# Second mixer's q, k and v as seven products of half matrices, with the residual parked in DRAM and all heads written out

## What is computed

```python
xn = rmsnorm(h, norm_mix[i])
proj = xn @ w_in                    # layer 1: 1024 -> 3 * 1024: q, k, v
q = proj[..., :1024].reshape(B, L, 8, 2, 64)
k = proj[..., 1024:2048].reshape(B, L, 8, 2, 64)
v = proj[..., 2048:].reshape(B, L, 8, 128)
q = partial_rope(_rms_f32(q, g_q), cos, sin) * 64 ** -0.5
k = partial_rope(_rms_f32(k, g_k), cos, sin)
p = softmax(q @ k.T)                # two maps per head
o = (p[0] - lam * p[1]) @ v
h = h + (_rms_f32(o, g_sub) * (1 - lambda_init)) @ w_out
h = h + (silu(xn2 @ w_gate) * (xn2 @ w_up)) @ w_down
```

## Time and profile before

| | before |
|---|---|
| median of the runs | 1862.98 us |
| profiled execution, span | 1860.4 us |
| TensorE busy | 1849.7 us (99%) |
| VectorE busy | 1235.1 us (66%) |
| ScalarE busy | 879.7 us (47%) |
| GpSimd busy | 1162.6 us (62%) |
| layer 0's FFN ends, mixer of layer 1 begins | at 905.6 us |
| mixer of layer 1, attention part | about 938 to 1326 us |

### The profile page before, as it was taken

One profiled execution on the slowest core, in us unless ns is written; L12 is line 12 of the kernel. 1 busy time (PEld: TensorE's weight loads), 2 busy tenths in 40 slices (PEclk: granted clock), 3 DMA queues, 4 the chain that ended last, 5 costly groups with the idle time before them and its releaser, 6 DMA issues.

```text
span 1860.4 us, 31456 instructions
## 1 busy us (share of the span) xinstructions
PE 1849.7 (99%) x10845; PEld 1742.0 (94%) x10845; DVE 1235.1 (66%) x2072; ACT 879.7 (47%) x1855; POOL 1162.6 (62%) x1533
## 2 busy tenths in 40 slices
PE   9999999999999999999999999999999999999999
PEld 8888889999999999999988888888889999999998
DVE  6756566768576757576876666666587575756663
ACT  6444343455444445454444444444465454444553
POOL 4453644468687878788843333333558788887885
PEclk9999999999999999999999999999999999999999
DMA  8789997549697977774475666664233535353534
GB/s 270 257 240 237 222 259 173 183 108 228 209 237 238 235 227 218 250 232 118 107 145 121 126 124 124 130 118 91 74 90 110 148 99 157 100 153 101 154 112 133
DMA packets 380153, 309.51 MB, mean 166 GB/s; under 512 B 14395, under 2 KB 322398, under 8 KB 379766
## 3 DMA queue, kind: packets, MB, share of 16 engines
q1 hardware_dynamic: 349472, 237.81, 42.1%
q0 software_dynamic: 28416, 69.21, 20.5%
q10 hardware_dynamic: 2134, 0.82, 0.2%
HBM read 302.16 MB, written 144.04 MB: 240 GB/s over the span
## 4 chain that ended last, share of the span: by engine, by line
PE 91%; DVE 5%; ACT 1%; issue 1%; DMA 1%; POOL 0%; SPq 0%; ACTq 0%; DVEq 0%; POOLq 0%
PE ps L974 51%; PE ps L884 26%; PE ps L1155 3%; PE ps L1312 3%; PE ps L1280 2%; PE ps L1302 1%; PE ps L1130 1%; PE ps L1214 1%; DVE rstd L1502 1%; PE ps L1164 1%; DVE sx L1554 0%; PE ps L1244 0%; DVE mx L2077 0%; DVE gt L1661 0%; DMA wk<-in_x_prompt_dram 0%
## 5 line engine op out<-in xcount | busy, mean ns | idle before, releaser
L974 PE MATMUL ps<-sx,wh 128*128 128x400 f32 (+1 forms) x2044 | 530.3, 340 | 0.9 <-POOL wl L808 0.5
L808 POOL TENSOR_TENSOR wl<-raw,wh 128x256 fp32r<-128x256 f32 (+1 forms) x432 | 355.6, 855 | 97.9 <-ACT wh L2243 96.4
L774 POOL CAST wh<-raw 128x256 fp32r<-128x256 f32 x248 | 102.5, 456 | 450.6 <-PE ps L884 424.9
L974 PEld LDWEIGHTS ps<-sx,wh 128*128 128x128 f32 x2044 | 373.4, 188 | 3.0 <-ACT gt_first L2258 0.9
L974 PE MATMUL ps<-sx,wl 128*128 128x400 f32 (+1 forms) x1022 | 347.6, 340 | 0.0
L808 POOL TENSOR_TENSOR wl<-raws,wh 128x256 fp32r<-128x256 f32 x328 | 283.8, 910 | 84.4 <-ACT wh L2243 84.0
L1715 DVE TENSOR_TENSOR h<-h,ps 128x400 f32<-128x400 f32 (+1 forms) x280 | 154.5, 559 | 131.5 <-PE ps L974 131.4
L974 PE MATMUL ps<-fx,wh 128*128 128x400 f32 (+1 forms) x904 | 235.3, 341 | 0.1
L884 PE MATMUL ps<-xh,wh 128*128 128x512 f32 (+1 forms) x752 | 211.2, 357 | 0.0
L884 PE MATMUL ps<-xl,wh 128*128 128x512 f32 (+1 forms) x752 | 207.3, 349 | 0.0
L778 POOL TENSOR_TENSOR wl<-raw,wh 128x256 fp32r<-128x256 f32 x248 | 198.8, 831 | 5.1
(11 more groups left out here) (330 smaller groups left out, 3552.0 us busy)
## 6 DMA issues: line engine op xcount, KB each, us to landing
in_sums<-in_ffn_w_in_dram SPq DMA_DIRECT2D x16, 1536.0 KB, 10.7
raw<-in_sums SPq DMA_DIRECT2D x96, 256.0 KB, 3.0
in_sums<-in_ffn_w_in_dram SPq DMA_DIRECT2D x16, 1280.0 KB, 7.2
raw<-in_ffn_w_in_dram SPq DMA_DIRECT2D x80, 256.0 KB, 3.0
raws<-in_sums SPq DMA_DIRECT2D x80, 256.0 KB, 3.1
raw<-out_sums SPq DMA_DIRECT2D x120, 128.0 KB, 2.6
raws<-in_ffn_w_in_dram SPq DMA_DIRECT2D x52, 256.0 KB, 3.1
raw<-in_m_w_in_dram SPq DMA_DIRECT2D x24, 512.0 KB, 4.8
```

The lines of the kernel that those rows point to most:

```text
L774: ins = pool.tensor_copy(wh[:, slot, c], raw[:, slot, c])
L808: ins = pool.tensor_tensor(slot_of(n, 1)[:, c], raw_of(n)[:, c], slot_of(n, 0)[:, c].bitcast(F32), ALU.subtract)
L974: mm = pe.matmul(product_bank(layer, s, j), slot_of(n, low_w)[:, k * P:(k + 1) * P], x, start=(j in OPENS and k + q == 0), stop=(k == tile ...
```

## The change

- **q, k, v.** The 24 blocks become 84 products (`mix_product`) of 12 matmuls of 128x400: seven for each of eight key-value jobs (k and v of one head are the two output halves) and seven for each of four query jobs (two heads). The first 14, key-value and query alternating, stand before attention; the rest in the 13 places of the heads by `HALVES`, a place counting half products of 6 matmuls.
- **Tokens.** `mix_part` takes the place of `high_and_square` and `low_and_squares`: for a tile of the lower four ScalarE makes a scaled copy and two highs, VectorE one sum and two lows; for its partner ScalarE a scaled copy and five highs, VectorE three sums and five lows. `axe`, `axo`, `an` are single buffers, so a pair waits for the pair before.
- **Weights.** Sums are made in DRAM during the FFN: 8 copies on SyncE, 8 accumulating DMAs on GpSimd. Eight of the copies for layer 1's FFN move into the mixer. Loads are 256 KB; there are four slots. For the first 14 products ScalarE makes the high parts (`mix_high`), afterwards GpSimd makes both.
- **Read-out.** Four of the seven products are copied out of PSUM by ScalarE (`mix_copy`), the others added by VectorE (`mix_add`). The root of the mean square is no longer applied to q and k. Instead epsilon is scaled by token: 14 small matmuls against `rstd` (`token_norms`), and one matmul more per head ahead of the square sums (`eps_sums`). v gets its root in `values`: eight activations in place of three.
- **Residual.** `h` is stored to DRAM tile by tile as its square is made (`keep_last`, eight stores of 400 KB); its tiles then hold q, `at` and the outputs of heads 0 to 5. ScalarE's `mix_high(4)` waits for all eight stores. In the last head six outputs are split again (`split_y`, six on ScalarE, six on VectorE), and the tiles of `h` are loaded back and awaited in `add_tile`.
- **Order.** All eight heads are written out. The three k tiles behind the first scores of head 0 are gone.

The core of the diff:

```diff
+KV_ORDER = (0, 3, 2, 1, 5, 4, 6)
+def made_in(hd):
+    i, steps = query_pair(hd + 2), [("kv", hd + 1, j) for j in KV_ORDER]
+    if hd % 2 == 0 and hd + 3 < D_HEADS:
+        return [*steps[0:6], ("q", i, 0), steps[6], ("q", i, 3), ("q", i, 2), ("q", i, 1)]
+    if hd % 2:
+        i = query_pair(hd + 1)
+        return [*steps[0:6], ("q", i, 5), steps[6], ("q", i, 4), ("q", i, 6)]
+    return steps
+MIX_ORDER = [(kind, 0, j) for j in KV_ORDER for kind in ("kv", "q")]
+N_FIRST = len(MIX_ORDER)
+for _hd in range(D_HEADS - 1):
+    MIX_ORDER += made_in(_hd)
+N_MIX = len(MIX_ORDER)
+MIX_PLACE = {x: m for m, x in enumerate(MIX_ORDER)}
+def split_query(kind, i):
+    return kind == "q" and i > 0
 ...
+HALVES = {"even": (2, 2, 1, 3, 2, 4, 2, 2, 1, 1, 0, 1, 1), "odd": (2, 2, 1, 3, 2, 4, 2, 2, 0, 1, 0, 1, 0),
+          "first": (1, 1, 1, 2, 2, 3, 2, 2, 1, 1, 0, 1, 1), "short": (2, 2, 1, 3, 2, 2, 2, 0, 0, 0, 0, 0, 0)}
+LATER_COPIES = {14 + 4 * i: 16 + i for i in range(8)}
+MIX_COPIES = {1: 0, 2: 1, 3: 2, 4: 3, 6: 4, 7: 5, 8: 6, 9: 7}
+MIX_ADDS = {(12, 0): 0, (13, 0): 1, (15, 0): 2, (17, 0): 3, (20, 0): 4, (21, 0): 5, (23, 0): 6, (25, 0): 7}
 ...
+    def keep_last(p):
+        sp.wait_ge(sq_ready, KT + 2 * p + 2)
+        for m in (p, p + KP):
+            sp.dma_start(h_last_kept[:, m, :], h[:, m, :]).then_inc(h_last_stored, 16)
 ...
+    for m in range(4):
+        mix_factor(m)
+        if m == 1:
+            keep_last(0)
+            keep_last(1)
+    keep_last(2)
+    for m in range(4, N_MIX):
+        mix_factor(m)
+        if m == 5:
+            keep_last(3)
+        if m in LATER_COPIES:
+            copy_for_sum(1, LATER_COPIES[m])
 ...
+    def mix_parts(m):
+        if m >= N_FIRST:
+            pool.wait_ge(mix_raw_in[m % 4], 16 * (m // 4 + 1))
+            pool.wait_ge(mix_done, m - 3)
+            for c in pieces(KP * P):
+                ins = pool.tensor_copy(mix_weight(m, 0)[:, c], mix_raw(m)[:, c])
+            ins.then_inc(mix_hi, 1)
+        pool.wait_ge(mix_hi, m + 1)
+        for c in pieces(KP * P):
+            ins = pool.tensor_tensor(mix_weight(m, 1)[:, c], mix_raw(m)[:, c], mix_weight(m, 0)[:, c].bitcast(F32),
+                                     ALU.subtract)
+        ins.then_inc(mix_split, 1)
 ...
+    def mix_product(x, k0=0, k1=KP, small=()):
+        (kind, i, j), m, small = x, MIX_PLACE[x], list(small)
 ...
+            pe.wait_ge(mix_split, m + 1)
+        for p in range(k0, k1):
+            if m < N_FIRST:
+                pe.wait_ge(axl_ready, ONCE + NPROD * p + j + 1)
+            for q, (low_w, low_x) in enumerate(((0, 0), (0, 1), (1, 0))):
+                mm = pe.matmul(ps[:, mix_bank(kind, i, j), 0:HT], mix_weight(m, low_w)[:, p * P:(p + 1) * P],
+                               sx[0][:, p * NPROD + j, low_x, :], start=(mix_opens(kind, i, j) and p + q == 0),
 ...
-        if first:
-            keys_block(0, 3)
+    for m in range(N_FIRST - 4):
+        mix_product(MIX_ORDER[m])
+        if m == 5:
+            token_norms()
 ...
+    for x in made_in(0)[0:2]:
+        mix_product(x)
+    attn_scores(0, 0, 0, first=True)
+    for hd in range(D_HEADS):
 ...
-        (s, j), m, c = LAST_TILES[i], LAST_ORDER[i], i + KT
-        sc.wait_ge(out_read, RANK[s, j] + 1)
-        sc.activation(xh[:, m, :], h[:, m, :], ACT.Copy,
-                      scale=par[:, MIXN + KT + m:MIXN + KT + m + 1]).then_inc(xh_ready, 1)
-        sc.wait_ge(sq_summed, c)
-        sc.activation(wk[:, 4, :], h[:, m, :], ACT.Square).then_inc(sq_ready, 1)
+    def mix_high(m):
+        if m < 4:
+            sc.wait_ge(prod_done, NF - MIX_FREE[m])
+        else:
+            sc.wait_ge(mix_done, m - 3)
+        sc.wait_ge(mix_raw_in[m % 4], 16 * (m // 4 + 1))
+        sc.activation(mix_weight(m, 0), mix_raw(m), ACT.Copy).then_inc(mix_hi, 1)
 ...
+    def mix_part(i):
+        if i == 0:
+            sc.wait_ge(pair_low, NPROD * NPAIR)
+            sc.wait_ge(prod_done, PLACE[in_job(FT - 1), 6] + 1)
+        elif not second:
+            sc.wait_ge(axl_ready, ONCE + NPROD * p)
+        dst = (axe, axo)[second]
+        sc.activation(dst[:, :], h[:, m, :], ACT.Copy,
+                      scale=par[:, MIXN + KT + m:MIXN + KT + m + 1]).then_inc(axf_ready, 1)
+        if i == KT - 1:
+            mix_high(3)
+        if not second:
+            sc.wait_ge(axf_ready, ONCE + i + 1)
+            high(B11, axe[:, a])
+            sc.wait_ge(atx_ready, ONCE + 4 * p + 1)
+            high(T1, an1[:, :])
+        else:
+            sc.wait_ge(atx_ready, ONCE + 4 * p + 2)
+            high(T2, an2[:, :])
+            sc.wait_ge(axf_ready, ONCE + i + 1)
+            high(B21, axo[:, a])
+            sc.wait_ge(atx_ready, ONCE + 4 * p + 3)
+            high(T3, axe[:, b])
+            high(B22, axo[:, b])
+            sc.wait_ge(atx_ready, ONCE + 4 * p + 4)
+            high(T4, axo[:, a])
+        sc.wait_ge(sq_summed, c)
+        sc.activation(asq[:, :], h[:, m, :], ACT.Square).then_inc(sq_ready, 1)
 ...
+        def low(j, src):
+            ve.wait_ge(axh_ready, ONCE + done + j + 1)
+            ve.tensor_tensor(sx[0][:, p * NPROD + j, 1, :], src, sx[0][:, p * NPROD + j, 0, :].bitcast(F32),
+                             ALU.subtract).then_inc(axl_ready, 1)
+        ve.wait_ge(axf_ready, ONCE + i + 1)
+        if not second:
+            ve.tensor_tensor(an1[:, :], axe[:, a], axe[:, b], ALU.subtract).then_inc(atx_ready, 1)
+            low(B11, axe[:, a])
+            low(T1, an1[:, :])
+        else:
+            ve.wait_ge(atx_ready, ONCE + sums + 1)
+            ve.scalar_tensor_tensor(an2[:, :], an1[:, :], -1.0, axo[:, b], ALU.mult, ALU.subtract).then_inc(atx_ready, 1)
+            ve.tensor_tensor(axe[:, b], axo[:, b], axe[:, b], ALU.subtract).then_inc(atx_ready, 1)
+            low(T2, an2[:, :])
+            low(B21, axo[:, a])
+            ve.wait_ge(atx_ready, ONCE + sums + 2)
+            ve.scalar_tensor_tensor(axo[:, a], an2[:, :], -1.0, axo[:, a], ALU.mult, ALU.subtract).then_inc(atx_ready, 1)
+            ve.wait_ge(atx_ready, ONCE + sums + 3)
+            low(T3, axe[:, b])
+            low(B22, axo[:, b])
+            ve.wait_ge(atx_ready, ONCE + sums + 4)
+            low(T4, axo[:, a])
+        ve.wait_ge(sq_ready, c + 1)
+        if i == 0:
+            ve.tensor_copy(rstd[:, :], asq[:, :]).then_inc(sq_summed, 1)
+        else:
+            ve.wait_ge(sq_summed, c)
+            ve.tensor_tensor(rstd[:, :], rstd[:, :], asq[:, :], ALU.add).then_inc(sq_summed, 1)
+    def mix_add(x):
 ...
+    def split_y(k):
+        ve.wait_ge(split_high, ONCE + k + 1)
+        ve.tensor_tensor(y_home(k, 1)[:, 0:TQ], h[:, Y_TILE[k], 0:TQ], y_home(k, 0)[:, 0:TQ].bitcast(F32),
+                         ALU.subtract).then_inc(yl_ready, 1)
```

703 lines of the change are left out of this document (471 added, 232 removed).

## The result

The change made the kernel slower: 1993.63 us (1987.89 to 2001.02) against 1862.85, a ratio of 1.0703 (95% interval 1.0677 to 1.0728). The forecast was 1886.5 with a range up to 1903. The sign was right and the size wrong more than fivefold: +131 us and not +24.

A forecast was written before the change was run, and what follows sets the result against it. TensorE, busy 1849.7 of 1860.4 us, was taken as the bound. Terms -19.9 + 18.5 + 4.5 + 12.5 + 5.9 + 2.0 = +23.5 gave a span of 1883.9, with 2.6 around it 1886.5 us; 8-in-10 range 1857 to 1903.

The forecast's parts named there:

- A: TensorE's own work: products save 23.9 us, small matmuls for token norms and epsilon add 2.0 each; -19.9 us.
- B: Hand-over from FFN to mixer: late VectorE additions, the fourth pair of tiles and stores delay product 4; +18.5 us.
- C: Start of attention: without three k tiles, maxima and exponentials are uncovered, and key squares join the path; +4.5 us (1 to 6).
- D: Ends of heads 0 to 6: VectorE's chain stays, TensorE has less work there and waits; +12.5 us (6 to 18).
- E: Last head: added output copies and subtractions mostly uncovered, first returning tile of `h` awaited; +5.9 us (4 to 7).
- F: TensorE's clock: idle stretches at the hand-over and head 6 lower it; +2 us (0 to 8).
- G: Items counted at nothing: GpSimd's DMA issues in the FFN, its mixer work, DMA room for copies; together 0 to 3 us.
- The rival on the faster side: Whole kernel: VectorE is not the limit, tail chains shrink below TensorE's work; -5.5 us, 1857.5 us; chance 0.19.
- Worse: Whole kernel: products also wait for weights, or the clock stays low through the hand-over; +41 us, 1904 us; chance 0.13.

## Why the prediction was wrong, step by step

The mixer's +74.6 can be put together. Its work is A, taken as it stood (-19.9). Idle time of TensorE rose from 1.2 to 43.8 us, +42.6. What is left, 51.9 us, is what TensorE's work took longer at the lower clock. The granted clock of the stretch says about the same: 0.10 of 532.8 us are 53, a part of which lies in idle time.

**A, TensorE's work: right, within what can be read.** In the kernel with the addition moved the clock held at 1.00 in four heads. There TensorE was busy for 44.8 us from one head's second scores to the next's in an odd head and for 46.9 in an even one, against 48.2 and 48.3 before. The sum gives 44.4 and 46.6 (three blocks out, ten or eleven products and 0.25 us for epsilon in). The token norms took 3.09 us against the 3.5 of the sum.

**B, the hand-over: the mechanism was right, its parts were not.** VectorE's last addition came 4.0 us behind the last FFN product, where 9.2 had been forecast. The three pairs took about 8.5, 10.5 and 8.7 us and not 9.7 each, which is 1.4 of the 5.2; 3.4 more come from TensorE itself, which reached the end of the FFN later, behind two waits on weights. (The sum also counted 15 additions to `h` from 877.9 us on; the trace of before has 18, which makes its own last addition 1.6 us later.) Three rows of VectorE, the last additions, the start of the fourth pair and its end, and ScalarE's high part behind the stores:

```profile
972.41 1.04 DVE L2045 TENSOR_TENSOR h<-h,ps 128x400 f32<-128x400 f32 x2
974.01 0.88 DVE L1924 TENSOR_TENSOR an<-axe 128x400 f32<-128x400 f32 x1 [0.55 <-ACT axe L2788]
...
982.17 0.98 DVE L1945 TENSOR_TENSOR rstd<-rstd,asq 128x800 f32<-128x800 f32 x1
```

```profile
981.27 0.86 ACT L2808 ACTIVATE asq<-h 128x800 f32<-128x800 f32 x1
...
988.65 0.63 ACT L2755 ACTIVATE wh<-raw 128x512 fp32r<-128x512 f32 x1 [6.53 <-DMA h_last_kept<-h]
```

The fourth pair took 9.1 us (974.01 to 983.15, forecast 9.7), the stores 6.5 from the end of the square (5.4), and product 4 began at 990.87, 21.5 us behind the FFN's end, not 27.3. Taking away the 8.8 us of products it is 12.7, some of it at the lower clock, and 3.4 us of waits on weights stand ahead of it in the FFN: 16 against 18.5.

In the fourth pair VectorE ran mostly at full pace, because GpSimd had little to do there. One row of GpSimd, in the fourth pair, and the four of VectorE that lie around its end:

```profile
977.67 2.20 POOL L1065 TENSOR_TENSOR wl<-raw,wh 128x256 fp32r<-128x256 f32 x2 [2.21 <-ACT wh L2755]
```

```profile
978.38 0.91 DVE L1919 TENSOR_TENSOR sx<-an,sx 128x400 fp32r<-128x400 f32 x1
979.21 1.10 DVE L1919 TENSOR_TENSOR sx<-axo,sx 128x400 fp32r<-128x400 f32 x1
980.23 0.56 DVE L1934 SCALAR_TENSOR_TENSOR axo<-an,axo 128x400 f32<-128x400 f32 x1
980.71 0.57 DVE L1919 TENSOR_TENSOR sx<-axe,sx 128x400 fp32r<-128x400 f32 x1
```

Beside the subtraction (977.67 to 979.87) two operations took 0.91 and 1.10 us, behind it 0.56. A loss is up to half a microsecond per operation. GpSimd lost as well: its two pieces took 2.20 us here and 1.73 in the same row at 965.82. The rule of the Trainium skill that was weighed there (SBUF — State Buffer, section SBUF: two separate sides) has the one that starts second wait until the first has ended. The trace agrees: both engines lost time where they met. But the losses, 0.35 and 0.54 us on VectorE and 0.47 on GpSimd, are parts of the other's operation and not the whole of it, as fits operations that start while the other is under way.

**C, the start: right.** 1.30 us for the key squares and 3.35 for the exponentials, 4.65 against 4.5.

**D, the ends of heads 0 to 6: too small, and in the wrong place.** TensorE was idle for 20.8 us there and not 12.5. Heads 0 to 5 have 16.7 us in place of 6.6: waits of up to 1 us at the key roots and the outputs, and in each head one of 1.6 to 2.0 us in the middle, on an addition that stood behind rope. The last was not seen at all: the order of VectorE was read for the tail and not for the banks that the products take turns in. Head 6 has 4.1 us against 5.9; by the sum's own numbers (a chain of 16.9 us less 10.1 of work) it should have been 6.8.

**E, the last head:** three waits of 4.31, 1.92 and 1.55 us, 7.8 against 5.9. The first two are on the outputs that are split again, 6.2 against the 4.4 of the sum. The third was put down to the tiles of `h` that come back; but it is there with 1.65 us in the kernel that loads none back, so this term was nothing.

**The total of B to E was right by luck.** B to E made 41.4 us, and idle time in the mixer rose by 42.6. But of that, B is 10.3 and not 18.5 (13.8 with the two waits in the FFN), C 4.65, D 20.8 and not 12.5, and E 7.8: B too large and D too small by the same 8 us. The measured time was missed by two other terms, F and G.

**F, the clock: +2 (0 to 8) was forecast, and about 52 us came in the mixer and 15 in the FFN.** This is the first step that failed, and it is the price that was wrong. It took the program's start for a scale, 2.0 us once, and counted two places. The runs show a price by idle time: 1.4 to 1.5 us for each us of waiting in the kernel before with VectorE late, and 2.2 in the changed kernel (94.5 us for 42.6, A taken as forecast). The Trainium skill (TensorE: Matmul & The Clock Gate, Part 1) has the rule that an idle TensorE falls back to 1.2 GHz and has to earn 2.4 again by work; the trace agrees, with matmuls 0.33 us apart behind a wait of 4.74 us. No row of before had a price for a wait in mid-kernel: TensorE was busy 99% of the time at a clock of 1.00. That called for a wide range beside 41 us of forecast waits, and the term had 8 us at most.

**G, at nothing: 0 to 3 was forecast, and 63.9 us came in the FFN.** This is the second step that failed. It looked at GpSimd's slack for issuing the DMAs, and at the DMA share in a head (0.60), and not at the DMA share of the stage in which the sums are made, 0.81 from 400 to 750 us. The added 24 MB, less what moved out, lifted it to 0.95. Of the 63.9 us the waits are 48.7 and the clock 15.2; without the added DMAs 59 of them were gone. (3.4 us of the waits are the two at the FFN's end, which belong to B.)

The rival on the faster side said that VectorE would not be the limit. VectorE was the limit: TensorE waited 4.7 us for the fourth pair and 11.5 us for the seven additions, all on VectorE. "Worse" named late weights and the clock, but only in the mixer and at +41.

What stays open: why the clock falls behind some waits of 1.6 us and holds behind others. In the changed kernel the fourth and fifth head (1194 to 1293 us) kept 1.00 with much the same waits as the other five, which had 0.73 to 0.94. So the price per microsecond is an average of these runs and not a rule. Also open is why copies and accumulating DMAs do little harm apart and much together. No version here beats the kernel before; the best, at 1928.9 us, is 3.5% slower. About 15 us of its mixer's idle time stood, little changed, in every version that computes the same result: the waits of the last head (7.6 us), the fourth pair of tiles (5.1) and the first exponentials (2 to 3).

## What to carry to other kernels

Where one engine is busy for 99% of the time at full clock, price a wait of that engine at one and a half to more than two times its length, and ask for each saving how many small waits it brings; 20 us of work saved here were worth nothing against forty of waits. Look at the DMA share of each stage that gets new traffic, not of the stage that the traffic is for, and at what stands beside the new transfers: in one FFN here 12 MB more of copies cost 8 us, and 12 MB of accumulating DMAs on top of them 51. And when an engine's instructions are put into a new order, follow every buffer that the busiest engine takes turns in to the place where it is freed; one addition behind two unrelated steps cost 28 us.

## What the runs showed of the hardware

- Three matmuls of 128x400 on fp32r operands take 0.55 us at the full clock and 1.00 at the lower one, 0.18 and 0.33 each.
- In the same stretch of 200 us of an FFN, the added plain copies alone left TensorE 0.1 us of idle time, the added accumulating DMAs alone 9.0, both together 37.9.
- The changed kernel scatters by 0.7% (1987.9 to 2001.0 us), the one before by 0.1% (1862.5 to 1864.3). Waits alone do not explain it: the kernel before with VectorE late has 24 us of them, and its two executions are 0.1 us apart.
- Waits of 2.6 to 3.9 us, eight of them and 24.4 us in all, lowered the granted clock of a 494 us stretch from 1.00 to 0.97.
- Matmuls of 112 columns on float32 operands, put into an idle stretch of 5.1 us, kept the clock at 2.4 GHz behind it.
- 2 MB from DRAM to DRAM took 14.9 us as a plain copy and 16.8 us as an accumulating one, while loads of 256 KB went on beside them. ScalarE waited up to 16.5 us for one of those loads, and SyncE took up to 10.4 us to issue one.
